# A page of 128 keys as 64 rows of 4 KB in one half of the partitions: decode attention of a hybrid trunk

## What is computed

```
k_past = cache_k[l][page_table].reshape(bs, past_len, A_HEADS, A_HEAD_DIM)
v_past = cache_v[l][page_table].reshape(bs, past_len, A_HEADS, A_HEAD_DIM)
f_past = cache_logf[l][page_table].reshape(bs, past_len, A_HEADS)
cum_f = jnp.cumsum(logf_all, axis=1)
s = jnp.einsum('bqhd,bkhd->bhqk', qi, k) * scale
s = s + fi.transpose(0, 2, 1)[..., :, None] - fk_t[..., None, :]
p = jax.nn.softmax(s, axis=-1)
out = jnp.einsum('bhqk,bkhd->bqhd', p, v)
```

## Time and profile before

| | us |
|---|---|
| median of 3 runs | 3415.62 (3413.36 to 3419.06) |
| the profiled execution | 3411.53 |
| its span, first to last instruction | 3409.8 |
| PE busy | 3172.3 (93%) |
| PE weight loads | 2453.1 (72%) |
| DVE busy | 1811.5 (53%) |
| ACT busy | 1414.4 (41%) |
| POOL busy | 1046.7 (31%) |

### The profile page before, as it was taken

The page is one execution under the profiler, slowest core; times in us unless marked ns, Lnnn a source line. Parts: engine busy times, 40 slices in busy tenths (PEclk is TensorE's granted clock), DMA queues, the critical chain, the costliest instruction groups (busy, mean ns, idle before and its releaser), DMA issues. The chain is left out here.

```text
span 3409.8 us, 58717 instructions
## 1 busy us (share of the span) xinstructions
PE 3172.3 (93%) x20175; PEld 2453.1 (72%) x20175; DVE 1811.5 (53%) x3174; ACT 1414.4 (41%) x2928; POOL 1046.7 (31%) x991
## 2 busy tenths in 40 slices
PE   7899999999999999999799999888888887999998
PEld 6678887788788778888577777555555555778787
DVE  4425556786756655655577777244444444444432
ACT  4412223454622474654577777423333333211222
POOL 2511313244354635140378788300000000222100
PEclk9899999999999999999799999999999999999999
DMA  7878778788879797878301212699999999554322
GB/s 271 303 232 270 238 253 261 245 317 281 290 253 326 235 304 240 279 235 237 107 14 51 56 39 78 233 383 384 386 386 385 386 384 331 203 167 161 136 88 82
DMA packets 425982, 810.44 MB, mean 238 GB/s; under 512 B 97709, under 2 KB 119125, under 8 KB 425706
## 3 DMA queue, kind: packets, MB, share of 16 engines
q1 hardware_dynamic: 413650, 799.67, 69.2%
q10 hardware_dynamic: 11488, 5.11, 0.6%
q0 software_dynamic: 576, 2.10, 0.2%
HBM read 674.11 MB, written 132.67 MB: 237 GB/s over the span
## 5 line engine op out<-in xcount | busy, mean ns | idle before, releaser
L1495 PE MATMUL prj_z_ps<-prj_w_hi,prj_h_ring 128*128 128x512 f32 x1792 | 722.5, 403 | 11.3 <-DMA prj_h_ring<-hops_scratch 6.9
L1497 PE MATMUL prj_z_ps<-prj_w_hi,prj_h_ring 128*128 128x512 f32 x1792 | 701.9, 392 | 0.0
L1496 PE MATMUL prj_z_ps<-prj_w_lo,prj_h_ring 128*128 128x512 f32 x1792 | 700.2, 391 | 0.0
L1940 POOL TENSOR_TENSOR pa_p_lo<-pa_probs,pa_p_hi 128x512 fp32r<-128x512 f32 (+1 forms) x320 | 367.6, 1167 | 110.7 <-ACT pa_p_hi L1952 106.9
L1495 PEld LDWEIGHTS prj_z_ps<-prj_w_hi,prj_h_ring 128*128 128x128 f32 x1792 | 338.2, 189 | 80.9 <-issue 8.0
L1497 PEld LDWEIGHTS prj_z_ps<-prj_w_hi,prj_h_ring 128*128 128x128 f32 x1792 | 337.3, 188 | 74.5
L2621 PE MATMUL sa_t_ps<-arena_ident,arena_k_raw 128*128 128x128 f32 x2048 | 280.6, 280 | 113.9 <-DMA arena_k_raw<-in_cache_k_dram 104.0
L1496 PEld LDWEIGHTS prj_z_ps<-prj_w_lo,prj_h_ring 128*128 128x128 f32 x1792 | 338.3, 189 | 66.2
L2501 DVE COPY sa_kT<-sa_t_ps 128x512 f32<-128x512 f32 x256 | 177.1, 692 | 358.0 <-PE sa_t_ps L2621 350.5
L2621 PEld LDWEIGHTS sa_t_ps<-arena_ident,arena_k_raw 128*128 128x128 f32 x2048 | 225.0, 142 | 166.2 <-DMA arena_k_raw<-in_cache_k_dram 135.5
L2445 ACT COPY sa_kT<-sa_t_ps 128x512 f32<-128x512 f32 x256 | 150.1, 586 | 445.5 <-PE sa_t_ps L2621 422.9
(11 more groups left out here) (416 smaller groups left out, 6250.0 us busy)
## 6 DMA issues: line engine op xcount, KB each, us to landing
prj_h_ring<-hops_scratch SPq DMA_DIRECT2D x448, 512.0 KB, 4.7
arena_k_raw<-in_cache_k_dram SPq DMA_DIRECT2D x512, 256.0 KB, 5.9
shared_v_early<-in_cache_v_dram SPq DMA_DIRECT2D x260, 256.0 KB, 5.9
sa_v_late<-in_cache_v_dram SPq DMA_DIRECT2D x252, 256.0 KB, 6.1
z_scratch<-prj_z_sb SPq DMA_DIRECT2D x224, 256.0 KB, 5.7
prj_raw<-in_w_main_dram SPq DMA_DIRECT2D x104, 256.0 KB, 6.0
arena_mg<-z_scratch SPq DMA_DIRECT2D x48, 512.0 KB, 5.2
hops_scratch<-prj_h_ring SPq DMA_DIRECT2D x32, 512.0 KB, 5.8
```

The source lines that it names most:

```text
L1495: pe.matmul(out, h[:, 0, k], hi, start=(k == 0), stop=False)
L1496: pe.matmul(out, h[:, 0, k], lo, start=False, stop=False)
L1497: mm = pe.matmul(out, h[:, 1, k], hi, start=False, stop=(k == HK - 1))
L1940: pool.tensor_tensor(p_lo[:, s % P_RING, 0:w], probs[:, s % P_RING, 0:w], p_hi[:, s % P_RING, 0:w].bitcast(F32), ALU.subtract).then_inc(pl ...
```

## The change

The shape of a page in the on-chip memory is changed, and all that depends on it:

- A page is read as 64 rows of two neighbouring keys, 4 KB each (`pages_of`). Page j of a chunk goes to partitions 0 to 63 if j is even and to 64 to 127 if it is odd, and takes the columns of two blocks (`page_in`). Block e of the pair then holds the keys of parity e of both pages.
- `kT` gets its blocks in the order of `block_of`, and `turn_weights` reads the weights by it. The number and the shape of PE's, ACT's and DVE's instructions stay.
- `decay_past` is stored in the order of `kT`: a chunk, 16 rows, 512 keys ordered by parity, pair of pages, page, key. For that DVE's last two wide subtractions write with the parities apart, and `store_past` issues 8 DMAs of 32 partitions in place of 2. The load of decays is then one run of 512 words in each of 16 partitions.
- SP waits for the turn of two old pages before it loads the even key page, and no more before the odd one.

```
+def pages_of(cache):
+    return cache.rearrange("l n (k e) h d -> (l n) k (e h d)", e=KEYS_EACH)
+def page_in(ring, slot, j):
+    rows = P // KEYS_EACH
+    at, first = slice(j % KEYS_EACH * rows, (j % KEYS_EACH + 1) * rows), j // KEYS_EACH * KEYS_EACH
+    return ring[at, slot, first:first + KEYS_EACH].rearrange("p e x -> p (e x)")
...
-                sp.dma_start(decay_past[pages, 0:HEADS], d_hi[:].bitcast(F32)).then_inc(past_stored, 16)
-                sp.dma_start(decay_past[pages, HEADS:2 * HEADS], cum[:]).then_inc(past_stored, 16)
+                for j in range(CHUNK_PAGES):
+                    a, b = divmod(j, KEYS_EACH)
+                    for half, src in enumerate((d_hi[:].bitcast(F32), cum[:])):
+                        sp.dma_start(dst[:, half * wide:(half + 1) * wide, a, b], src[j:P:CHUNK_PAGES].rearrange(
+                            "c h (e k) -> c (h e) k", e=KEYS_EACH)).then_inc(past_stored, 16)
...
-                        dve.tensor_tensor(d_hi[:], wide, cum[:], ALU.subtract).then_inc(past_step, 1)
+                        dve.tensor_tensor(apart(d_hi[:]), each, in_turn(cum[:]), ALU.subtract).then_inc(past_step, 1)
...
+        def block_of(j):
+            at = j % KEYS_EACH * (CP // KEYS_EACH) + j // KEYS_EACH
+            return slice(at * PAGE, (at + 1) * PAGE)
...
                 for j in range(CP):
-                    sp.wait_ge(turned, (g - RING) * CP + (j + 1))
-                    page(pages[j], j, k_raw[:, slot], k_view, k_loaded[slot])
+                    if j % KEYS_EACH == 0:
+                        sp.wait_ge(turned, (g - RING) * CP + (j + KEYS_EACH))
+                    page(pages[j], page_in(k_raw, slot, j), k_view, k_loaded[slot])
```

More of the change, by code:

```diff
@@ L39 @@
 CHUNK_PAGES = 4
+KEYS_EACH = 2
 CHUNKS = N_PAGES // CHUNK_PAGES
@@ L1659, in attend_prompt @@
     IN_GROUP = P // N_PAGES
+    PAST_STORE = 2 * CHUNK_PAGES * 16
     with ExitStack() as stack:
@@ L1809, in store_past @@
             def store_past(group):
-                pages = slice(group * P, (group + 1) * P)
+                chunks, wide = P // CHUNK_PAGES, HEADS * KEYS_EACH
                 sp.wait_ge(past_step, 3 * group + 3)
-                sp.dma_start(decay_past[pages, 0:HEADS], d_hi[:].bitcast(F32)).then_inc(past_stored, 16)
-                sp.dma_start(decay_past[pages, HEADS:2 * HEADS], cum[:]).then_inc(past_stored, 16)
+                dst = decay_past[group * chunks:(group + 1) * chunks].rearrange("c h (e a b k) -> c (h e) a b k", a=CHUNK_PAGES // KEYS_EACH,
+                                                                               e=KEYS_EACH, b=KEYS_EACH)
+                for j in range(CHUNK_PAGES):
[3 more added lines that the diff above has]
+                            "c h (e k) -> c (h e) k", e=KEYS_EACH)).then_inc(past_stored, 16)
             def load(h):
@@ L1877, in _ @@
             sp.wait_ge(stored, 16 * (HEADS // 2 - 1 + GROUPS))
-            sp.wait_ge(past_stored, 16 + 32 * (HEADS // 2))
+            sp.wait_ge(past_stored, 16 + PAST_STORE * (HEADS // 2))
         @block.gpsimd
@@ L2048, in past @@
                             dve.wait_ge(gathered, pair * 16 + 16)
-                            dve.wait_ge(past_stored, pair * 32 + 16)
+                            dve.wait_ge(past_stored, pair * PAST_STORE + 16)
                         by_head = lf[:].rearrange("p (k h) -> p h k", h=HEADS)[:, j]
@@ L2055, in past, with in_turn, apart @@
                     wide = rest[:].unsqueeze(2).broadcast_to([P, HEADS, PAGE])
+                    each = rest[:].unsqueeze(2).unsqueeze(3).broadcast_to([P, HEADS, PAGE // KEYS_EACH, KEYS_EACH])
+                    def in_turn(x):
+                        return x.rearrange("p h (k e) -> p h k e", e=KEYS_EACH)
+                    def apart(x):
+                        return x.rearrange("p h (e k) -> p h k e", e=KEYS_EACH)
                     if (g, j) == (2, 0):
@@ L2065, in past @@
                     if (g, j) == (3, 11):
-                        dve.tensor_tensor(d_hi[:], wide, cum[:], ALU.subtract).then_inc(past_step, 1)
+                        dve.tensor_tensor(apart(d_hi[:]), each, in_turn(cum[:]), ALU.subtract).then_inc(past_step, 1)
                     if (g, j) == (3, 13):
                         dve.wait_ge(past_step, pair * 3 + 2)
-                        dve.tensor_tensor(cum[:], log_rest, d_hi[:].bitcast(F32), ALU.subtract).then_inc(past_step, 1)
+                        dve.tensor_tensor(apart(cum[:]), in_turn(log_rest), apart(d_hi[:].bitcast(F32)), ALU.subtract).then_inc(past_step, 1)
                 def maximum(self, h, u):
@@ L2345, in find, with page @@
                 return page_numbers(nc, table[0:1, bass.ds(chunk * CP, CP)], n_pool)
-            def page(at, j, dst, view, sem):
-                sp.dma_start(dst[:, j], view[bass.ds(at, 1)].rearrange("a k x -> (a k) x")).then_inc(sem, 16)
+            def page(at, dst, view, sem):
+                sp.dma_start(dst, view[bass.ds(at, 1)].rearrange("a k x -> (a k) x")).then_inc(sem, 16)
             def load_k(g, slot, pages):
                 for j in range(CP):
-                    sp.wait_ge(turned, (g - RING) * CP + (j + 1))
-                    page(pages[j], j, k_raw[:, slot], k_view, k_loaded[slot])
+                    if j % KEYS_EACH == 0:
+                        sp.wait_ge(turned, (g - RING) * CP + (j + KEYS_EACH))
+                    page(pages[j], page_in(k_raw, slot, j), k_view, k_loaded[slot])
             def load_v(w, slot, pages, first=False):
@@ L2358, in load_v @@
                         sp.wait_ge(weighed, (w - V_RING) * 2 + (1 if j == 0 else 2))
-                    page(pages[j], j, v_of(slot), v_view, v_loaded[slot])
+                    ring, at = (shared.v_early, slot) if slot < RING else (v_late, slot - RING)
+                    page(pages[j], page_in(ring, at, j), v_view, v_loaded[slot])
             def load_both(g, slot, first=False):
```

23 lines of the change are left out of this document (10 added, 13 removed).

## The result

The changed kernel takes 3731.6 us (median of 4 runs, 3712.9 to 3760.3) against 3415.8 for the kernel before on the same chip. The ratio is 1.093, with an interval of 1.090 to 1.096. It is slower by 9%, as forecast in direction. 3848 us was forecast, and the range of 3650 to 4060 holds the result. The profiled execution took 3716.6 us, its span 3714.8, which is 305 us more than the 3409.8 of before.

The account below looks back on a forecast made before the run. It took the page stream, for which PE waits, as the bound. Alternating halves +430 and the end +2 made +432 us on the profiled 3411.5, 3843.5; the median 4.1 above gave 3848 us, range 3650 to 4060 (8 in 10).

Parts of the forecast that it names:

- What bounds: Sample attention loop: PE waits for key pages, 61.9 us per 400, and everyone else waits for PE.
- Packets: Page stream: 4 KB pieces taken alone give 422 GB/s against 385, up to 10%, 74 us less than 706.
- side by side: Rival for the page stream: the two halves run beside each other, -74 us, 3345 us; chance 8%.
- faster: Whole kernel: chance that it gets faster by over 0.2%, put at 8%.
- Two halves in turn: Loop's page stream: pages alternating between partition halves run at 235 GB/s, 1136 us in place of 706, +430 us.
- partly out of step: Rival for the page stream: engines drift half of the way, 310 GB/s, +155, 3571 us; chance 10%.
- the forecast's own bounds of 3745 to 3965: Whole kernel: bounds around 3848 us, from keeping both 258 and 213 GB/s for the stream; chance 69%.
- the rival that the clock falls to 1.2 GHz throughout: Loop: PE at the low clock needs about 9.9 us a chunk, +532, 3948 us; chance 10%.
- SP's waits and the decay blocks: Loop: waiting for two turned pages and loading decays in 2 KB pieces were each counted as zero.
- Decay stores and DVE: Stage before the loop: smaller decay stores and two-key-step subtractions, each 0 to +5 us, taken as zero.
- the stages before 2100 us: Everything ahead of the loop: expected within 5 us of the kernel before.
- The end: After the last keys: the last value pages, 1 MB, land in 4.5 us in place of 2.7, +2.

Follow-up runs that it names:

- Experiment 2: Changed kernel, but two pages come as one DMA of 128 rows of 4 KB over all partitions (wrong rows read): 3399.4 us, ratio 0.9952 to the kernel before.
- experiment 5: Changed kernel, but a page goes to every second partition, even or odd, in place of one half: 3492.6 us, ratio 1.022 to the kernel before.
- experiments 1 to 3: Changed kernel with pages on all partitions in 2 KB pieces, 3424.2 us; on all in 4 KB pieces, 3399.4 us; on halves in 2 KB pieces, 3706.6 us.
- experiment that set engines apart (8): Changed kernel plus one DMA before the loop, 8 separate rows of 16 KB from memory to memory: 3679.2 us, ratio 1.077 to the kernel before.
- Experiment 1: Changed kernel with pages on all 128 partitions in 2 KB pieces again, all other edits kept: 3424.2 us, ratio 1.0021 to the kernel before.

## Why the prediction was right, and where its sizes were off

**What bounds.** Right. The loop of the sample attention was on the page stream and still is, now with 128.0 of PE's 129.5 idle microseconds per 400 on key pages.

**Packets.** The sign was right, the size was not. I took 422 GB/s from two microseconds of decay stores, up to 10% over 385. Experiment 2 has 396 in a long stream, 3%. A burst of 2 us of another kind (stores, not loads) was a poor row for a stream. The rival "side by side" used it, and its 3345 us would have been too low by some 50: experiment 2, the nearest to it, has 3399. That rival was out of reach for another reason as well: it needs a chunk in 5.05 us, and SP's instructions alone take 5.8 (experiment 5). The prediction read SP from its issues, 2.7 to 3.0 us a chunk, and left out the register work and the read of page numbers between them and the longer issue of the new shape. It cost the forecast nothing, because the stream needs more; the 8% for "faster" were too many.

**Two halves in turn.** This is the term that carried the sum, and the mis-sized one. I took 235 GB/s between 213 and 258; the loop has 268, so the term is +288 us and not +430. The value was right for the start: 238 GB/s in 2200 to 2250, after which the rate wandered up to 314 and back to 260. I wrote that an engine's lead lasts only for a burst and that in a stream I expect the later values. The mean of the stream lies above both ends of my price, 213 and 258, so a burst was the wrong row for a long stream. A reading that fits is that a stream of 1000 pages gives engines time to drift apart and a burst doesn't; no run shows that drift. I had it as the rival "partly out of step" at 310 GB/s and 3571 us; the result lies between it and the forecast, nearer to the forecast (3732 is 116 from 3848 and 161 from 3571). It lies outside the forecast's own bounds of 3745 to 3965, to which I gave 69%. Only the wider range holds it, which had been drawn towards that rival; to that extent it was luck.

**The cause.** Half of the partitions as such, not the size of pieces, is confirmed by experiments 1 to 3 (383, 396 and 274 GB/s). That it is one half, not 64 partitions, is shown by experiment 5 (349). That what hurts is all engines on one half in the same moments is supported by the series in how long one half is held, per engine if 16 engines share a page of 256 KB: 32 KB gives 249 GB/s, 16 KB gives 266, both halves at hand from two queues 295. It isn't shown outright: the one experiment that set engines apart (8) did not bring the rate up. What exactly they wait for in each other stays open.

The Trainium skill's page SBUF — State Buffer was the right one to ask. Its section Door 1: The DMA port swizzle says that the low half lies behind half of the ports, and experiment 5, where a page reaches both halves, agrees: by the rule of that section every second partition reaches all the ports, and the run has 349 GB/s with SP as a bound. Its section "Can I just issue two DMAs to hit both halves?" gives 6% for two DMAs side by side. The store of the earlier trace rows had 199 GB/s at a busy share of 0.92, which would be some 225 at the 1.04 of the stream, an estimate. Against that, halves in turn had 238 at first, 6% more, and the trace agrees with the page there; 268 in the mean of the loop is 20% more, and 295 from two queues some 32% more (at 1.03 the store would have 223). Its warning holds, its number doesn't carry over to a long stream; the measurement decides.

**The clock.** I gave 10% to the rival that the clock falls to 1.2 GHz throughout. It read 0.88 in the mean of the loop, between the two levels of 2.4 and 1.2 GHz, and PE was busy 69% of the stretch (682.04 of 994). PE's busy time in the loop grew with it, from 587.57 us to 682.04, while DVE's and ACT's stayed (297.75 and 210.08). As forecast, PE did not become the bound: the DMA share stayed at 1.03 and PE's idle time is nearly all wait for pages.

**SP's waits and the decay blocks, zero.** Experiment 1 has both and keeps 383 GB/s, so zero was right.

**Decay stores and DVE, 0 to +5 each.** Rows of the changed kernel (ns min/median/max, first to last start):

```profile
L2093 DVE TENSOR_TENSOR pa_d_hi<-pa_rest,pa_cum x4: 3152/3152/3153, 1737.2 to 2104.1; 128x1024 fp32r<-128x1024 f32 x4
...
L2096 DVE TENSOR_TENSOR pa_cum<-pa_lf,pa_d_hi x4: 2267/2272/2273, 1741.0 to 2107.9; 128x1024 f32<-128x1024 f32 x4
...
L1831 SPq DMA_DIRECT2D dpast_scratch<-pa_d_hi x16: 592/632/675, 1743.3 to 2114.2; - x16
...
L1865 SPq DMA_DIRECT2D arena_k_raw<-in_cache_k_dram x12: 468/472/513, 2121.3 to 2129.6; - x12
...
L2651 PE MATMUL sa_t_ps<-arena_ident,arena_k_raw x2048: 272/273/478, 2172.4 to 3177.9; 128*128 128x128 f32 x187
...
PE pa_max_ps L2191 <- DVE pa_part_max L2102: 9.5, 19, 1.1
```

The subtractions went from 2.35 and 1.52 us to 3.15 and 2.27, which is 4 x 1.6 = 6 us of DVE. The last row is PE's wait for DVE's maxima from 1700 to 2170. The row of before is:

```profile
PE pa_max_ps L2164 <- DVE pa_part_max L2075: 4.4, 10, 1.0
```

So some 5 us of the 6 reach PE, at the place that the prediction named for it; in the nine experiments, which all have this edit, the wait is 8.4 to 9.5. I had taken 0 and kept +5; the value should have been +5. The stores take SP 8 x 0.63 = 5 us per group, and the first keys are issued 15.8 us later than in the earlier trace rows; PE's first use, at 2172.4, is still 43 us behind the last of those issues, so they cost nothing. PE's first use came 11 us later than the 2161.4 of before: 5 are DVE's, and 5.5 are there already when the first changed subtraction begins (1737.2 against 1731.7), ahead of any changed work; over the kernels of this study that start moves between 1730.8 and 1739.1. So the stages before 2100 us moved by more than the 5 us that I allowed: the last of these subtractions begins at 2104.1 in place of 2094.4.

**The end.** +5 us measured, +2 forecast.

In sum: 288 + 12 + 5 = 305 us, where +432 was forecast. The one rate was 142 us too dear, the other terms 15 too cheap.

## What to carry to other kernels

Before a tile is loaded in larger pieces by giving it fewer partitions, find the rate of a transfer to exactly those partitions in the trace: here pieces of 4 KB in half as many DMAs were worth 3%, and one half of the partitions cost 30% of the stream. Pages in turn to both halves don't cure that, whether from one queue or from two; spreading each page over both halves does most of it. And find the time of the issuing engine for one round of its loop, not only that of its issues: a new shape can make it the next bound. A rate from a burst of one or two microseconds is a price for a burst: for a long stream take its value as one end of the range, not as the middle.

## What the runs showed that I had not expected

- The rate of the stream to alternating halves isn't steady. With the same code in every chunk it goes from 238 to 314 GB/s and back to 260 within 400 us, while a page over every second partition has 345 GB/s in the first 100 us and 349 in the 400 after.
- Wide pages between half pages lose their rate too (237 GB/s in all), so a mixture can be worse than either.
- Issuing a page of 64 rows takes SP 468 ns where one of 128 rows took 332, and 598 with two pieces per row. In the changed kernel it is covered: with all that stands between the issues SP needs 5.8 us of a chunk of 7.95 (994 / 125). In experiment 5 it isn't.

```profile
L2378 SPq DMA_DIRECT2D arena_k_raw<-in_cache_k_dram x500: 468/468/1354, 2174.5 to 3161.8; - x167
```

- DVE's subtraction of two [128 x 1024] tiles of 4-byte words costs 0.8 us more when its operands are walked with a step of two keys (3152 against 2348 ns, and 2272 against 1516).
- The one DMA here whose 8 rows of 16 KB lay in one piece came as 16 packets of 8 KB or more, not as 8; with gaps between the rows it came as 8.
